# The first block's closing norm and the loads behind it in one block, and up-projection weights stored by chunk

## The reference

```
def _conv_ffn(h, w_up, conv_w, conv_b, w_down):
    u = _causal_dwconv(h @ w_up, conv_w, conv_b)      # w_up: 1024 x 5632
    a, val = jnp.split(u, 2, axis=-1)
    return (jax.nn.gelu(a) * val) @ w_down            # w_down: 2816 x 1024

def first_block(x, ...):
    for l in range(2):
        ...
        x = x + g1 * _mixer(h, ...)
        h = _rmsnorm(x, norm_ffn_w[l]) * (1 + sc2) + sh2
        x = x + g2 * _conv_ffn(h, ffn_w_up[l], ffn_conv_w[l], ffn_conv_b[l], ffn_w_down[l])
    return _rmsnorm(x, final_norm_w)

def second_block(x, c, ctx, ...):   # mixers over x and a context of 256 tokens, then a mixture of experts
    ...
```

## Time and profile before

| | |
|---|---|
| median of 3 runs | 2504.11 us (2504.09 to 2507.25) |
| the profiled execution | 2500.94 us, span 2499.1 us |
| TensorE matmul busy | 2026.5 us (81%) |
| VectorE busy | 1448.5 us (58%) |
| ScalarE busy | 1109.2 us (44%) |
| mean granted TensorE clock | 0.889 of full |
| transfers on SP's queue | 445.42 MB, 50.1% of 16 DMA engines' span |

### The profile page before, as it was taken

The page is one execution under the profiler, slowest core; times in us unless marked ns, Lnnn a source line. Parts: engine busy times, 40 slices in busy tenths (PEclk is TensorE's granted clock), DMA queues, the critical chain, the costliest instruction groups (busy, mean ns, idle before and its releaser), DMA issues. The chain is left out here.

```text
span 2499.1 us, 38021 instructions
## 1 busy us (share of the span) xinstructions
PE 2026.5 (81%) x15206; PEld 1708.6 (68%) x15206; DVE 1448.5 (58%) x1787; ACT 1109.2 (44%) x1308; POOL 144.2 (6%) x134
## 2 busy tenths in 40 slices
PE   4688888598878888689758985798629999999997
PEld 3586666597767666589647774686527878788785
DVE  0274424586436343477425857854438878788786
ACT  0262422464254332356316434212216767677674
POOL 0000000000000000000000632630000000000000
PEclk9898789798989788889878997798759999999999
DMA  8742454453364245264423220000147979899796
GB/s 330 281 148 76 135 187 176 137 201 106 115 226 131 81 160 219 76 212 160 160 78 126 70 73 9 13 18 10 68 140 289 377 281 374 303 350 375 282 370 240
DMA packets 196927, 447.60 MB, mean 179 GB/s; under 512 B 10656, under 2 KB 58400, under 8 KB 196768
## 3 DMA queue, kind: packets, MB, share of 16 engines
q1 hardware_dynamic: 196768, 445.42, 50.1%
HBM read 444.33 MB, written 1.05 MB: 178 GB/s over the span
## 5 line engine op out<-in xcount | busy, mean ns | idle before, releaser
L208 DVE TENSOR_TENSOR me_wlow<-me_w,me_whigh 128x2048 fp32r<-128x2048 f32 x195 | 442.6, 2289 | 98.6 <-ACT me_whigh L203 98.2
L203 ACT ACTIVATE me_whigh<-me_w 128x2048 fp32r<-128x2048 f32 x195 | 372.1, 1919 | 121.0 <-PE ps L216 120.7
L208 DVE TENSOR_TENSOR mix_wlow<-mix_w,mix_whigh 128x1024 fp32r<-128x1024 f32 (+2 forms) x116 | 140.1, 1213 | 155.6 <-ACT mix_whigh L203 155.5
L214 PE MATMUL ps<-me_whigh,me_xhigh 128*128 128x512 f32 x512 | 207.5, 405 | 16.7 <-PEq L115 16.7
L214 PE MATMUL ps<-up_xhigh,up_whigh 128*128 128x256 f32 x704 | 203.0, 288 | 17.8 <-DVE up_wlow L208 17.7
L215 PE MATMUL ps<-me_wlow,me_xhigh 128*128 128x512 f32 x512 | 201.9, 394 | 0.0
L215 PE MATMUL ps<-up_xlow,up_whigh 128*128 128x256 f32 x704 | 201.8, 287 | 0.0
L216 PE MATMUL ps<-me_whigh,me_xlow 128*128 128x512 f32 x512 | 201.7, 394 | 0.0
L216 PE MATMUL ps<-up_xhigh,up_wlow 128*128 128x256 f32 x704 | 201.6, 286 | 0.0
L203 ACT ACTIVATE mix_whigh<-mix_w 128x1024 fp32r<-128x1024 f32 (+2 forms) x116 | 121.2, 1047 | 142.9 <-DMA mix_w<-w_mix 115.3
L214 PEld LDWEIGHTS ps<-up_xhigh,up_whigh 128*128 128x128 f32 x704 | 137.6, 195 | 19.3 <-issue 16.1
(11 more groups left out here) (664 smaller groups left out, 4399.7 us busy)
## 6 DMA issues: line engine op xcount, KB each, us to landing
me_w<-w_exp_gate SPq DMA_DIRECT2D x34, 2048.0 KB, 9.7
me_w<-w_exp_up SPq DMA_DIRECT2D x34, 2048.0 KB, 10.1
me_w<-w_exp_down SPq DMA_DIRECT2D x32, 2048.0 KB, 10.2
mix_w<-w_mix SPq DMA_DIRECT2D x108, 512.0 KB, 4.0
mix_w<-ada_w SPq DMA_DIRECT2D x96, 512.0 KB, 5.2
up_w<-ffn_w_up SPq DMA_DIRECT2D x40, 1024.0 KB, 7.2
ada_w<-ada_first SPq DMA_DIRECT2D x12, 2048.0 KB, 22.5
sec_w<-w_in SPq DMA_DIRECT2D x31, 512.0 KB, 3.6
```

What stands on the lines that cost most here:

```text
L203: return nc.scalar.activation(high, x, ACT.Copy)
L208: return nc.vector.tensor_tensor(low, x, high.bitcast(F32), ALU.subtract)
L214: nc.tensor.matmul(out, lh, rh, start=start, stop=False)
```

## The change

Two edits, which do not touch each other. The first stores `ffn_w_up` by chunk: on the host, before the launch, the columns are brought into the order of the chunks and each chunk is laid out by partition, so that one partition's 8 x 512 numbers (16 KiB) lie together. A chunk is then one transfer, a piece of the first chunk one transfer of 4 KiB a partition, and the semaphore counts halve. The second puts the load of `final`, the norm, and the loads of `rows`, `second_vectors`, the masks and `consts2` into one block, `first_output`.

```
-    w = layer_in("ffn_w_up").rearrange("(k p) n -> p k n", p=P)
+    w = layer_in("ffn_w_up").rearrange("j p (k n) -> j p k n", k=KD)
...
-                            for s in range(2):
-                                c0 = s * D_FF + j * pairs * P
-                                sp.dma_start(raw[:, j % STAGES, a:b, s * pairs * P:(s + 1) * pairs * P],
-                                             w[:, a:b, c0:c0 + pairs * P])\
-                                    .then_inc(first[n] if j == 0 else landed[j % STAGES], 16)
+                            sp.dma_start(raw[:, j % STAGES, a:b, :], w[j, :, a:b, :])\
+                                .then_inc(first[n] if j == 0 else landed[j % STAGES], 16)
...
-            load(core, "final", [(final[:, :], I["final"].to_broadcast([P, DM]))])
-            inverse_rms(core, "final_rms", [x[:, t, :] for t in range(TT)], rstd, junk, DM)
-            with core.stage("final") as (block, own):
...
+def first_output(core, I, x, coming):
...
+        with nc.Block(no_gpsimd_drain=True) as block:
+            @block.sync
+            def _(sp):
+                sp.dma_start(final[:, :], I["final"].to_broadcast([P, DM])).then_inc(final_here, 16)
+                for dst, src in coming:
+                    sp.dma_start(dst, src).then_inc(here, 16)
+                sp.wait_ge(here, 16 * len(coming))
+
+            @block.scalar
+            def _(act):
+                for t in range(TT):
+                    if t:
+                        act.wait_ge(squared, t)
+                    nc.scalar.activation(junk[:, :], x[:, t, :], ACT.Square, accum_out=rstd[:, t:t + 1]).then_inc(squared, 1)
+                act.wait_ge(meaned, 1)
+                nc.scalar.activation(rstd[:, :], rstd[:, :], ACT.Sqrt).then_inc(rooted, 1)
+
+            @block.vector
+            def _(dve):
+                dve.wait_ge(squared, TT)
+                nc.vector.tensor_scalar(rstd[:, :], rstd[:, :], 1.0 / DM, EPS, ALU.mult, ALU.add).then_inc(meaned, 1)
+                dve.wait_ge(rooted, 1)
+                nc.vector.reciprocal(rstd[:, :], rstd[:, :]).then_inc(inverted, 1)
+                dve.wait_ge(inverted, 1)
+                dve.wait_ge(final_here, 16)
+                for t in range(TT):
+                    nc.vector.scalar_tensor_tensor(out=x[:, t, :], in0=x[:, t, :], scalar=rstd[:, t:t + 1],
+                                                   in1=final[:, :], op0=ALU.mult, op1=ALU.mult).then_inc(scaled, 1)
...
-                    load(core, "masks", [(masks[:, d, :], I["masks"][d]) for d in range(2)] + [(ct[:, :], I["consts2"])])
+                    first_output(core, I, x, [(fvt[:, :], I["second_vectors"]), (masks[:, 0, :], I["masks"][0]),
+                                              (masks[:, 1, :], I["masks"][1]), (ct[:, :], I["consts2"]), rows])
```

More of the change, by code:

```diff
@@ L1908, in split @@
                             if j == 0:
-                                act.wait_ge(first[n], 32)
+                                act.wait_ge(first[n], 16)
                             elif n == 0:
-                                act.wait_ge(landed[j % STAGES], 32 * (j // STAGES + (j % STAGES > 0)))
+                                act.wait_ge(landed[j % STAGES], 16 * (j // STAGES + (j % STAGES > 0)))
                             if j >= STAGES and n == 0:
@@ L2101, in first_block @@
             core.settle()
[L2102 to L2105, removed]
-            load(core, "final", [(final[:, :], I["final"].to_broadcast([P, DM]))])
-            inverse_rms(core, "final_rms", [x[:, t, :] for t in range(TT)], rstd, junk, DM)
-            with core.stage("final") as (block, own):
[L2109 to L2113, removed]
+def first_output(core, I, x, coming):
+    nc = core.nc
+    with ExitStack() as mem, core.section() as sem:
+        rstd, junk, final = (core.sb(mem, n, [P, w]) for n, w in (("rstd", TT), ("junk", DM), ("final", DM)))
+        final_here, here, squared, meaned, rooted, inverted, scaled = (sem(n) for n in (
+            "final_here", "second_here", "final_squared", "final_meaned", "final_rooted", "final_inverted", "final_scaled"))
+        with nc.Block(no_gpsimd_drain=True) as block:
[24 more added lines that the diff above has]
+                                                   in1=final[:, :], op0=ALU.mult, op1=ALU.mult).then_inc(scaled, 1)
@@ L3993, in _, with second_block @@
                     add_back(j).then_inc(added, 1)
-def second_block(core, I, k, mod, x):
+def second_block(core, I, k, mod, x, rows):
     nc = core.nc
@@ L4005, in second_block @@
         tile_d = nc.dram_tensor("tile_slots", [TILES + 1, P, TT], F32).ap()
-        load(core, "second", [(fvt[:, :], I["second_vectors"])])
         with ExitStack() as mix:
@@ L4086, in build @@
         rows = core.sb(ctx, "rows", [P, n_rows])
-        load(core, "rows", [(rows[:, :], I["rows"].to_broadcast([P, n_rows]))])
         second_block(core, I, dict(ident=ident, ones=ones[:, :], b_r=rows[:, R_OFF["b_rg"][0]:R_OFF["b_re"][1]],
-                                   **{n: rows[:, a:b] for n, (a, b) in R_OFF.items()}), mod_next, x)
+                                   **{n: rows[:, a:b] for n, (a, b) in R_OFF.items()}), mod_next, x,
+                     (rows[:, :], I["rows"].to_broadcast([P, n_rows])))
         with core.stage("stored") as (block, stored):
@@ L4214, in layouts @@
     d["first_vectors"], d["next_vectors"] = vectors[0], np.stack(vectors[1:])
+    both = [w.reshape(DM, 2, FF_TILES // 2, 2 * P).transpose(0, 2, 1, 3).reshape(DM, -1) for w in d["ffn_w_up"]]
+    d["ffn_w_up"] = np.stack([w.reshape(KD, P, -1, 4 * P).transpose(2, 1, 0, 3).reshape(-1, P, KD * 4 * P) for w in both])
     d["ada_first"] = modulation_pieces(a["ada_w"][0])
```

## The result

Over six executions each, the changed kernel took 2477.85 us in the median (2470.39 to 2482.36) and the kernel before 2501.62 us (2495.68 to 2507.25). The ratio is 0.9902, with a 95% interval of 0.988 to 0.9925: about 24 us less, between 19 and 30. The profiled execution of the changed kernel took 2470.39 us, the fastest of the six.

The account below looks back on a forecast made before the run. TensorE bounds the feed-forward part, the up-projection's start waits for weights, and the first block's end is a line of short waits. Saving 14.0 + 4.0 = 18.0 us gives 2482.9 us profiled, 2486 us for the median; range 2480 to 2494.

Parts of the forecast that it names:

- the time of queued transfers: Merged block: loads queued one behind another take 1.7 us fixed plus 7.2 us moving data, 8.9 us.
- The fit of the Trainium skill: Merged block: about 2.0 us fixed plus bytes over 436 GB/s, 7.1 us for six loads, saving 15.8 us.
- The rival that `final` comes last: Merged block: transfers share the engines evenly, `final` lands with the rest; 11.5 us saved, 2488.6 us in all; chance 0.07.
- so the first piece lands at 469.8: First layer's up-projection start: one transfer takes 3.3 us, not 4.2 us, to land; first matmul at 472.2.
- The second step: Up-projection start: at 400 GB/s or so a piece lands each 1.3 us, what TensorE takes for its six matmuls.
- The third: Up-projection starts: 2.0 and 3.25 us won; the clock decides what stays, middle 1.5 and 2.5 us, together 4.0 us.
- The slower rival: Up weights in mid-run: rows 16,384 bytes apart make the load the bound; 54 us more, 2558 us; chance 0.05.
- The rival that the layout is worth nothing: Up-projection start: first-transfer latency binds or the clock rises later; only the block's 14.0 us saved, 2490 us; chance 0.14.
- the median of the runs stands 3.2 us higher; against it I predict 2486 us: Whole kernel: profiled 2500.94 us less 18.0 gives 2482.9; the runs' median is 3.2 us higher, so 2486 us.
- the clock steps of later blocks ... can shift either end by 2 or 3 us: Later blocks: clock steps may fall elsewhere, widening the likeliest case's 2482.9 to 2491 and layout-at-zero's 2493.7 to 2480 to 2494.
- Theory A: In the experiments: the edits save what the touched stretches show, some 18 us; the rest is scatter of single executions.
- theory B: In the experiments: more is saved than the touched stretches show, 24 us, because stretches behind them also run faster.

Follow-up runs that it names:

- the kernel that idles longer: Kernel before, with the load of `final` made five times in five blocks; 2512.25 us against 2497.16, ratio 1.0062.
- short rows: Kernel before with up weights stored by chunk, but fetched in two transfers a chunk with rows of 1 KiB; 2505.55 us, ratio 1.0006.

## Why the prediction was right and wrong

**The merged block: mechanism right, size near.** The load-by-load line of waits went as described, the norm didn't wait for anything else, and the transfers ended last. The sum said 9.3 us from `final` to the context and 14.0 us saved; three profiles of the changed kernel gave 10.2, 10.1 and 9.3, and the two of the block alone 10.2 and 10.1. The term that was too small in two of the three is the time of queued transfers, 8.9 us in the sum and about 9.7, 9.6 and 8.8 us in the profiles: I took `final`'s landing alone (3.3 us) also for `final` with others behind it, which took 4.8, 4.4 and 4.0. The fit of the Trainium skill, "DMA: Bandwidth & Descriptors", section "Anatomy of one DMA", which the prediction sets beside its sum, is given there for transfers that GpSimd issues, and these are SP's; its 7.1 us would have been further off. The rival that `final` comes last was wrong: it landed at about 1277.1, long before `rows`, and cost VectorE 0.91 us off the path. The scaling ended 2.8 us before the next block instead of about 2.

**The up weights: the sum near, two of its steps wrong.** I predicted 4.0 us and the first two traces give 1.8 + 3.2 = 5.0 us, 4.4 averaged over all of them. That it came so near is in part luck, because two errors offset each other. The step "so the first piece lands at 469.8", 0.9 us sooner, failed: the first piece came 4.39 and, in the second layer, 4.09 us behind its issue, as before, and the first matmul 6.85 and 6.55 us behind it, not 5.7. It may be the same misreading as above, which no run separates: `final` alone in the queue was the pattern, and a piece has three pieces and a chunk behind it. The second step, the pieces behind it each 1.3 us, was right (1.23 us in the first layer, 1.2 to 1.6 in the second). The third, how much remains, was taken at the middle between "clock rises at the same moment" and "rises as much earlier as the work does". In fact it rose 2.84 us earlier relative to the issue in the first layer (12.11 instead of 14.95 by the rows at 475.01 and 481.41), though unit 0 ended only 0.97 us earlier (12.11 instead of 13.08), and 4.05 us earlier in the second (10.81 instead of 14.86). So it came after 24 and 19 matmuls where it had come after 33 and 26, and this made up for the late first piece. The whole gain is made there: at 0.12 us a matmul, the changed kernel reaches its 34th matmul of the first layer at 13.19 us, 1.8 us sooner, and the 27th of the second at 11.65, 3.2 us sooner, which are the gains of the two stretches.

In every trace with whole pieces the first matmul of 0.28 us came 3.8 to 5.5 us behind the first matmul, and 7.1 to 11.2 us behind it in every trace with two transfers a piece, where TensorE has gaps between the pieces. That the clock follows TensorE's unbroken work is what these rows suggest; no run here varies the gaps by themselves.

**The slower rival** had no ground: SP still waits for VectorE in mid-run, 91.2 us in 9 waits in place of 82.7, so chunks with 16 KiB rows arrive earlier, not later; two late chunks are still split 11.52 us apart, and ScalarE waits for no chunk after chunk 1. SP's own waits, changed kernel, 462 to 615 us:

```profile
SPq L1877 <- DVE up_wlow L208: 91.2, 9, 11.0
```

The Trainium skill, "DMA: Bandwidth & Descriptors", section "Latency and other measured facts", warns of pitches of 512 KiB and more; at 16 KiB the trace shows no such loss. **The rival that the layout is worth nothing** falls too by the stretches (139.4 to 140.1 in the eight stretches of four traces with the layout, against 141.6 to 142.6 in eight without it), although the timed runs of the layout alone could not tell it from nothing.

**The time: outside the range, by 2 us.** The median of 2477.85 us stands 8 us below the predicted 2486. The sum of 18.0 us agrees with the 18.2 of the touched stretches, so the mechanism isn't what missed. The step that failed is the one from the sum to the time and the range: "the median of the runs stands 3.2 us higher; against it I predict 2486 us", and "the clock steps of later blocks ... can shift either end by 2 or 3 us". I had three executions of before, 2504.09 to 2507.25, and took them for the kernel's scatter. Over the 47 executions of before that the comparisons rest on (6, 26 and 15), the mean is 2499.3 us and they lie between 2487.59 and 2515.83. The 2 or 3 us for later blocks were an estimate without a row, and they went almost wholly to the lower end of the range; untouched stretches differed by up to 16 us between single traces. The starting point was nearly 5 us too high, and a median of six of such executions moves by several us on its own. From 2499.3, the same sum gives 2481 us, inside the range. The other 3 us of the miss are the part of the timed difference that the touched stretches don't show.

Is the effect 18 or 24 us? Pooled means, with 95% intervals from the scatter of the executions: changed 2477.8 (18 executions), before 2499.3 (47), difference 21.5 +- 2.9 (24.4, 22.4 and 18.1 us in the three groups of runs); merged block alone 2485.3 (16), 14.0 +- 3.8 less than before, beside 13.2 to 13.3 in its stretch; the layout beside the merged block 7.5 +- 3.9, alone 1.6 +- 3.9, beside 5.0 in its stretches. All stretches' values lie within these but the sum, 18.2, which is some 0.4 us short of the interval's end. Theory A missed its expectation for the median in two of two repetitions; theory B, that later stretches run faster because less idle time lies ahead of them, got no support from the kernel that idles longer. A remainder of some 3 us between stretches and timed means may be chance; it stays open.

## What to carry to other kernels

Where loads and short computations alternate in blocks that all engines must leave together, their waits add up though nobody is busy: here 23.4 us for 2.2 MB and a norm, 10 in one block. Cost a queued transfer from a row where others stand behind it, not from one that had the queue alone. And measure an edit of under 1% by the stretches that it touches, in several traces, and ask first how far an untouched stretch moves from trace to trace; with three executions of before, the scatter is not known yet.

## What the hardware showed that I had not expected

`final`, 512 KB, landed after 3.3 to 3.7 us when alone (eight times: once in the kernel before, in the layout alone and with short rows, five times with longer idleness), and after 4.0 to 4.8 us when it was first of a queue (eight profiles); the memory moved 86 to 220 GB/s for one or two us after the first transfer, before it came to 400 and more.

The mean granted clock of one and the same program, before, lay between 0.881 and 0.896 over 41 executions, low in the slowest (2515.83 us at 0.881) and high in the fastest (2487.59 us at 0.893, 2487.78 at 0.896). From trace to trace the untouched stretches moved by up to 7 us in 466 (462.9 to 470.1) and 16 us in 1190 (1185.5 to 1201.2). Of the 15.5 us between the shortest and the longest of the three rows of "rest" above, 12.8 are TensorE's busy time.
